# Four conditioning rows of the dense layer's scale summed by GpSimd, in a decoder trunk of two layers

## The reference, cut to what matters

```python
c_act = jax.nn.silu(c)
for l in range(DEPTH):
    mod = (c_act @ w_mod[l] + b_mod[l])[:, None, :]
    sh1, sc1, g1, sh2, sc2, g2 = jnp.split(mod, 6, axis=-1)
    h = x * (1.0 + sc1) + sh1
    y = hybrid_mixer(h, ...)
    x = layer_norm(DN_ALPHA * x + (1.0 + g1) * y, ln_g[l, 0], ln_b[l, 0])
    h = x * (1.0 + sc2) + sh2
    y = swiglu(h, ...) if l % 2 == 0 else moe_swiglu(h, ...)
    x = layer_norm(DN_ALPHA * x + (1.0 + g2) * y, ln_g[l, 1], ln_b[l, 1])
```

## Time and profile before

| what | value |
|---|---|
| median of 3 runs | 1275.26 us (1275.22 to 1275.42) |
| the profiled execution's own time | 1272.66 us |
| span of the profiled execution | 1270.9 us |
| granted TensorE clock, mean over the span | 0.983 |
| busy time of PE | 1183.0 us (93%) |
| busy time of DVE | 569.0 us (45%) |
| busy time of ACT | 302.1 us (24%) |
| busy time of POOL | 43.8 us (3%) |

### The profile page before, as it was taken

The page is one execution under the profiler, slowest core; times in us unless marked ns, Lnnn a source line. Parts: engine busy times, 40 slices in busy tenths (PEclk is TensorE's granted clock), DMA queues, the critical chain, the costliest instruction groups (busy, mean ns, idle before and its releaser), DMA issues.

```text
span 1270.9 us, 26228 instructions
## 1 busy us (share of the span) xinstructions
PE 1183.0 (93%) x11180; PEld 641.1 (50%) x11180; DVE 569.0 (45%) x913; ACT 302.1 (24%) x521; POOL 43.8 (3%) x84
## 2 busy tenths in 40 slices
PE   1889889999999898799999999999999999999996
PEld 1879867788878787523334323334233233333332
DVE  6799988677758999421021020111210210210224
ACT  0557243433336571310010010100100100100100
POOL 2101010000011010000000000000000000000001
PEclk9899989999999999799999999999999999999998
DMA  9973868899727648889999989999989999999950
GB/s 340 312 257 116 290 227 312 322 347 329 244 68 239 201 167 315 334 326 371 413 364 414 394 299 414 412 364 411 388 310 411 410 364 404 396 362 411 379 233 34
DMA packets 149083, 403.60 MB, mean 318 GB/s; under 512 B 19964, under 2 KB 71328, under 8 KB 137696
## 3 DMA queue, kind: packets, MB, share of 16 engines
q1 hardware_dynamic: 146720, 395.16, 82.5%
q0 software_dynamic: 2240, 6.68, 1.4%
HBM read 400.75 MB, written 1.05 MB: 316 GB/s over the span
## 4 chain that ended last, share of the span: by engine, by line
PE 75%; DVE 13%; DMA 6%; issue 3%; ACT 2%; SPq 1%; POOL 0%; DVEq 0%; ACTq 0%
PE bank L1349 36%; PE bank L1368 18%; PE bank L337 5%; PE bank L339 4%; PE bank L338 4%; DVE mod_acc L1541 3%; DMA raw_u<-in_ffn_w_up_dram 2%; DMA u_raw<-in_w_in_dram 2%; DVE u_low L1552 2%; PE bank L1331 1%; DMA mod_first<-in_w_mod_dram 1%; PE bank L1228 1%; DVE score L1596 1%; PE bank L1339 1%; PE bank L1022 1%
## 5 line engine op out<-in xcount | busy, mean ns | idle before, releaser
L1349 PE MATMUL bank<-raw_w,xg 128*32 128x512 f32 (+1 forms) x4608 | 462.9, 557 | 4.5 <-issue 2.5
L1349 PEld LDWEIGHTS bank<-raw_w,xg 128*32 128x32 f32 x4608 | 147.1, 110 | 304.7 <-issue 304.6
L1368 PE MATMUL bank<-raw_w,heT 128*32 128x512 f32 x2112 | 232.9, 593 | 0.0
L1915 DVE TENSOR_TENSOR he<-he,bank 128x256 f32<-128x256 f32 (+1 forms) x72 | 25.6, 384 | 369.4 <-ACT he L869 369.4
L869 ACT ACTIVATE he<-bank 128x256 f32<-128x256 f32 (+1 forms) x72 | 21.2, 367 | 542.8 <-PE bank L1349 542.8
L1368 PEld LDWEIGHTS bank<-raw_w,heT 128*32 128x32 f32 x2112 | 67.3, 110 | 150.5 <-issue 149.3
L1942 DVE SCALAR_TENSOR_TENSOR ycat<-bank,gate_tab,ycat 128x512 f32<-128x512 f32 x36 | 25.4, 747 | 173.0 <-PE bank L1340 171.1
L1541 DVE SCALAR_TENSOR_TENSOR mod_acc<-mod_row,c_act,mod_acc 128x1024 f32<-128x1024 f32 x70 | 89.8, 1283 | 6.8 <-DVE mod_acc L1541 0.9
L337 PE MATMUL bank<-u_high,hT_H 128*128 128x256 f32 x256 | 75.4, 294 | 4.9 <-DVE u_low L1552 3.5
L339 PE MATMUL bank<-u_high,hT_L 128*128 128x256 f32 x256 | 72.8, 284 | 0.0
L338 PE MATMUL bank<-u_low,hT_H 128*128 128x256 f32 x256 | 72.6, 284 | 0.0
(11 more groups left out here) (284 smaller groups left out, 1378.7 us busy)
## 6 DMA issues: line engine op xcount, KB each, us to landing
raw_w<-in_moe_w_down_dram SPq DMA_DIRECT2D x88, 1024.0 KB, 8.6
raw_w<-in_moe_w_gate_dram SPq DMA_DIRECT2D x128, 512.0 KB, 8.5
raw_w<-in_moe_w_up_dram SPq DMA_DIRECT2D x128, 512.0 KB, 9.8
mod_row<-in_w_mod_dram SPq DMA_DIRECT2D x80, 512.0 KB, 6.4
raw_w<-in_moe_w_gate_dram SPq DMA_DIRECT2D x64, 384.0 KB, 5.6
raw_w<-in_moe_w_up_dram SPq DMA_DIRECT2D x64, 384.0 KB, 6.8
u_raw<-in_w_in_dram SPq DMA_DIRECT2D x20, 1024.0 KB, 7.5
raw_d<-in_ffn_w_down_dram SPq DMA_DIRECT2D x11, 1024.0 KB, 10.1
```

What stands on the lines that cost most here:

```text
L1349: last = mm(bank[g][32 * q:32 * q + 32, 0:2 * HALF[c]].rearrange("s (m j r) -> s m j r", m=2, r=64), xg[:, i, k, 32 * g:32 * g + 32], cols ...
L1368: last = mm(bank[3 + g][32 * q:32 * q + 32, :], heT[(par + c) % 2][:, g, 2 * a + b, :], W[:, b, h * 512:(h + 1) * 512], start=(c == 0 and ...
L1915: V.tensor_tensor(h, h, bank[g][:, w:2 * w].rearrange("s (j c b) -> s j b c", b=2, c=32), ALU.mult).then_inc(s["m_hid"], 1)
```

## The change

GpSimd gets an accumulator of its own, `pool_acc`, of 128 x 1024, at a place where the first mixer keeps the attention probabilities and the dense layer its converted down weights. After the two RMS powers GpSimd waits until the second attention product has been made, and then takes rows 16 to 19: row 16 with one product by a scalar into `pool_acc`, rows 17 to 19 each with a product in place and a sum of two tiles. The product and the sum are separate instructions, with a semaphore between them.

VectorE leaves rows 16 to 19 out. Row 20 becomes the first of its accumulator (a product by a scalar) and counts for five rows in `row_rd`; rows 21 to 23 follow as before.

TensorE waits for the four rows of GpSimd before the scale's sum over partitions, and adds both accumulators there: 128 small products instead of 64, in pairs, the second of each pair added in PSUM.

SP waits, before it loads the weights of dense step 2 into `gu_in1`, also for the scale's sum over partitions (`mod_ps` at 4).

```diff
--- before.py
+++ after.py
@@ -84,6 +84,7 @@
 GATES = {2: 0, 9: 1, 10: 2, 11: 3}
 MOD_ROWS = [(m + FIRST_MOD, l, a, k) for m, (l, a) in enumerate(MODS) for k in range(KT)]
 ROWS_DENSE, ROWS_MIX1 = 24, 64
+POOL_ROWS = range(16, 20)
 ROWS_AT_STEP = (0, 5, 5, 5, 5, 4, 4, 4, 4, 4, 0)
 MOD_AT_STEP = {3: 5, 5: 6, 6: 7, 8: 8}
 
@@ -279,6 +280,8 @@
         last_S = place("last_S", [P, GROUPS, T], at=hTH_at)
         y_last = place("y_last", [P, GROUPS, 512], at=hfull_at)
 
+        pool_acc = place("pool_acc", [P, D], at=over + 40 * 1024)
+
         score, dsel, prob, relu = [score0, score1], [dsel0, dsel1], [prob0, prob1], [relu_a, relu_b]
 
         xH0 = place("xH0", [P, D], F32R, at=rows_at)
@@ -302,7 +305,7 @@
             yT_ps yT_H yT_L mv rstd x_n g3 stored
             f_guH f_guL f_gu f_silu f_hid f_t f_tH f_tL f_dH f_dL f_d
             rt_ps lg8 expd sel rank_ps npass lg_rd xb_ps xsplit xsplitL G xg_ps xg
-            m_used m_silu m_hid m_tH m_oS m_st m_S m_sc m_acc m_y0 m_y1 m_yH m_yL m_end""".split():
+            m_used m_silu m_hid m_tH m_oS m_st m_S m_sc m_acc m_y0 m_y1 m_yH m_yL m_end pool_rd""".split():
             s[name] = sem("s_" + name)
         row_ld = [sem(f"s_row_ld{i}") for i in range(NROWBUF)]
         mod_ld = row_ld + [sem(f"s_mod_ld{i}") for i in range(NROWBUF, len(FIRST_ROWS))]
@@ -442,6 +445,7 @@
                     sp.wait_ge(s["proj"], NU)
                 elif q == 2:
                     sp.wait_ge(s["row_rd"], 22)
+                    sp.wait_ge(s["mod_ps"], 4)
                 else:
                     sp.wait_ge(s["f_guL"], 2 * (q - 2))
                 b = (q + 1) % 2
@@ -604,6 +608,18 @@
             pool.wait_ge(s["mod_sum"], 2)
             gate_bias(0, 2, g_row)
             mixer(0)
+            pool.wait_ge(s["pv_ps"], 2)
+            for r in POOL_ROWS:
+                m, l, a, k = MOD_ROWS[r]
+                row = mod_row[0][ROW_BUF[r]]
+                pool.wait_ge(row_ld[ROW_BUF[r]], row_landed(r))
+                if k == 0:
+                    last = pool.tensor_scalar(pool_acc[:], row[:], c_act[:, 0:1], None, ALU.mult)
+                else:
+                    link(pool.tensor_scalar(row[:], row[:], c_act[:, k:k + 1], None, ALU.mult))
+                    pool.wait_ge(s["pool_rd"], k)
+                    last = pool.tensor_tensor(pool_acc[:], pool_acc[:], row[:], ALU.add)
+                last.then_inc(s["pool_rd"], 1)
             norm_power(0)
             gate_bias(0, 5, g_row)
             pool.wait_ge(s["x_ln"], 2)
@@ -980,10 +996,12 @@
             pe.wait_ge(s["stage_ld"], 32)
             nc.tensor.transpose(bank[7][:, 0:P], stage[:], ident[:]).then_inc(s["stageT"], 1)
 
-            def sum_chunk(acc, o):
+            def sum_chunk(acc, o, more=None):
 
                 for k in range(KT):
-                    last = mm4(o[:, k:k + 1], acc[:, k * P:(k + 1) * P], ones[:, 0:1], start=True, stop=True)
+                    last = mm4(o[:, k:k + 1], acc[:, k * P:(k + 1) * P], ones[:, 0:1], start=True, stop=more is None)
+                    if more is not None:
+                        last = mm4(o[:, k:k + 1], more[:, k * P:(k + 1) * P], ones[:, 0:1], start=False, stop=True)
                 return last
             pe.wait_ge(s["mod_sum"], 1)
             sum_chunk(ycat[:, 1, :], bank[6][:, KT:2 * KT])
@@ -1189,7 +1207,9 @@
                         if l == 0 and i == 2 + t:
                             m = i + 1
                             pe.wait_ge(s["row_rd"], (m - 1) * KT)
-                            sum_chunk(mod_acc[m % 2], bank[3 * t][:, 0:KT]).then_inc(s["mod_ps"], 1)
+                            if t:
+                                pe.wait_ge(s["pool_rd"], len(POOL_ROWS))
+                            sum_chunk(mod_acc[m % 2], bank[3 * t][:, 0:KT], pool_acc if t else None).then_inc(s["mod_ps"], 1)
                         elif l and t and i == 2:
                             pe.wait_ge(s["row_rd"], len(MOD_ROWS))
                             gate_sum(11, (0, 3))
@@ -1532,15 +1552,15 @@
                     row, acc = mod_row[int(n >= ROWS_MIX1)][ROW_BUF[n]], mod_acc[m % 2][:]
                     dve.wait_ge(row_ld[ROW_BUF[n]], row_landed(n))
                     if n:
-                        dve.wait_ge(s["row_rd"], n)
-                    if k == 0:
+                        dve.wait_ge(s["row_rd"], n if n - 1 not in POOL_ROWS else POOL_ROWS[0])
+                    if k == 0 or n - 1 in POOL_ROWS:
                         if m >= 4:
                             dve.wait_ge(s["mod_ps"], m - 2)
-                        last = V.tensor_scalar(acc, row[:], c_act[:, 0:1], None, ALU.mult)
+                        last = V.tensor_scalar(acc, row[:], c_act[:, k:k + 1], None, ALU.mult)
                     else:
                         last = V.scalar_tensor_tensor(out=acc, in0=row[:], scalar=c_act[:, k:k + 1], in1=acc,
                                                       op0=ALU.mult, op1=ALU.add)
-                    last.then_inc(s["row_rd"], 1)
+                    last.then_inc(s["row_rd"], 1 + len(POOL_ROWS) if n - 1 in POOL_ROWS else 1)
 
             def low_unit(l, u):
 
@@ -1750,7 +1770,7 @@
                 condition_rows(range(72, 76) if l else range(12, 16))
                 gate_apply(10 if l else 2, (1, 2), g_row)
                 low_unit(l, NIN + 3)
-                condition_rows(range(76, 80) if l else range(16, 24))
+                condition_rows(range(76, 80) if l else range(20, 24))
                 if l == 0:
                     dve.wait_ge(s["mod_ps"], 3)
                     conditioning(0, 3, bank[0][:, 0:KT]).then_inc(s["modT"], 1)
```

## The result

| | before | after |
|---|---|---|
| median of 5 runs | 1275.22 us | 1280.97 us |
| range of the runs | 1274.76 to 1275.42 | 1280.80 to 1284.34 |
| profiled execution, span | 1270.9 us | 1279.1 us |

The ratio is 1.0055, with a 95% interval of 1.0042 to 1.0068: slower by 5.4 to 8.7 us; 5.75 us between the medians, and 7.0 us by the ratio, which takes in that two of the five runs took 1284 us. I had forecast slower, by 3.4 us, and at most 5.2. The two spans lie 8.2 us apart, which is more than the medians do; single executions of the kernel before took from 1272 to 1279 us, so I read stages, and take off a shift of 0.39 us that the profile of after has before the stage begins.

What follows compares the result with a forecast made beforehand. VectorE's chain almost alone bounds the edited stage. Three products and three sums on its path, 3.2 + 6.3 - 0.5 - 5.56, give +3.4 us, small terms nothing: 1278.7 us on the median, range 1272.7 to 1280.4.

Steps and rivals of the forecast that it cites:

- VectorE's wait for the scale: Before tile 1: scale ready at 165.8, VectorE asks at 168.0, so hidden by 2.2 us and no wait.
- What is saved on VectorE: Scale's row steps on VectorE: four steps of 1.39 us go, 5.56 us saved.
- the rival without hindrance: GpSimd and VectorE don't hinder each other; TensorE's w_out end sets tile 1: -2.5 us, 1272.8; chance 0.22.
- the end of TensorE's products: Last w_out unit before the scale's sum: without hindrance TensorE's products are done at 160.4 and limit the gain.
- What its instructions cost: GpSimd's rows 16 to 19: four products of 1.06 us and three sums of 2.1 us, 10.5 us in all.
- Turns: VectorE and GpSimd alternate reading SBUF, whoever starts first holding the interface for its whole instruction: likeliest +3.4 us; chance 0.50.
- The small terms: Around the scale's sum: 64 more products (0.71 us) hidden; SP's wait, row 20's wait and GpSimd's queue cost nothing.
- SP's new wait: Before the load into gu_in1: scale's sum at 165.8 precedes SP's arrival at 167.2, so it costs nothing.
- The rest of the program: Behind the edited stage, from TensorE's last dense product on: nothing found that would absorb a few microseconds.
- VectorE always wins: Rival: VectorE isn't delayed, GpSimd's last sum ends near 166, tile 1 starts at 168.1: +3.0 us, 1278.3; chance 0.08.
- a quick sum: Rival: GpSimd's sum of two tiles takes 1.06 us like its product: +0.3 us, 1275.6; chance 0.18, shared with partial hindrance.

Runs made afterwards that it cites:

- run 5: The change without GpSimd's part and the sum's second half, rows 16 to 19 left out of the scale; against the kernel before, ratio 0.9974, -3.3 us.
- run 1: The kernel before once more, no edit, with a second profile; its span was 1273.4 us, 2.5 us over the first.
- run 2: Kernel before with VectorE and TensorE unchanged, GpSimd making the four products and three sums for nobody; ratio 1.0063, +8.0 us.
- run 3: Kernel before with GpSimd making seven fills of 128 x 1024 beside VectorE instead of products and sums; ratio 1.0000.
- run 9: The change with both accumulators summed by halves, so TensorE has as many products as the kernel before; against that kernel, ratio 1.0026, +3.3 us.
- run 6: The change with two rows (16 and 17) on GpSimd instead of four; against the kernel before, ratio 1.0031, +4.0 us.
- run 8: The kernel before with TensorE adding `mod_acc` twice in the scale's sum; ratio 1.0017, +2.2 us.
- run 4: The kernel before with two products by a scalar and two sums of two tiles at GpSimd's start, on own tiles; one execution took 1276.36 us.
- run 12: Against the kernel before: rows 16 and 17 on TensorE by halves, shift and scale summed by halves, scale's sum between tile 1's w_out units; ratio 0.9970, -3.8 us.

## Why the prediction was wrong

The direction was right, the size not: +5.75 us between the medians (7.0 by the ratio, interval 5.4 to 8.7) against +3.4, and above my range by 0.6. Two terms that I had put at nothing make up the difference: VectorE's wait for the scale, and the experts' loop.

*What is saved on VectorE:* right. In run 5 row 12 to the end of row 23 took 13.81 us instead of 19.25, 5.44 less, with 0.22 us of waiting for row 23 instead of a step's 0.1. Its -3.3 us meets the -2.5 of the rival without hindrance with 0.7 us of the sum off, but partly by luck: the end of TensorE's products, which I had fixed at 160.4, moved by 1 us there, and it moves by as much between two traces of the kernel before (run 1).

*What its instructions cost:* both mis-sized. The sum is 2.34 us for my 2.1. The product is 2.87 us for my 1.06, which I took from the rate of the affine select; 18.5 us of work instead of 10.5, so GpSimd ended at 165.1.

*Turns:* right in kind (runs 2 and 3), and nearly in size: VectorE lost 8.3 us for my 9.0. The product's length and hold are different things: it holds VectorE for 0.7 us only, where I charged nearly all of its 1.06 (and the fourth, beside row 20, for 0.85). Two errors met, and that the total came out near is luck: an instruction nearly three times as long, and a hold of two thirds of what I charged. The last sum then ran beside tile 0's residual instead of a row. The net +3.4 of this term stands against +2.8 in the trace up to tile 0's statistics and +3.3 (1.9 to 4.6) in run 9.

*The small terms:* here it failed. I had the scale's sum "ready at 165.8", hidden by 2.2 us, since 64 products more take 0.71 us. They took about that (127 of the 128 in 1.2 us), and then TensorE stood still for 2.39 us. With the products' later end (165.1 for 164.3; the 72 took 11.4 us at a granted clock of 0.74, where my sum had 10.3) the scale came at 169.0 and VectorE waited 1.33 us. SP's new wait did bind, but by little: the load into gu_in1 was issued at 169.10, 4.0 us behind the w_out products, where run 9, with its sum long over, issued it 3.6 us behind them. What these 0.4 us cost is open.

*The rest of the program:* not in my sum at all. "I find nothing behind it that would absorb a few microseconds" asked what would take the loss away, not what would add to it. The 64 counted products more, ahead of the experts' loop, cost 2.3 us inside it. Three kernels with 11244 counted products (the change, runs 6 and 8) have the step, 2.3 to 2.7 us over the two passes; those with 11180 (the kernel before and runs 1, 2, 3, 4, 5, 9 and 12) stay within -0.3 and +0.6 us of the kernel before. Kernels with 11436 have none either, and the one with 11148 gains 1.5 us a pass and loses 2.4 later. So more products don't simply cost more; that it is the place of the loop in TensorE's program is argued, not shown. That the loss comes from how instructions are fetched is a likely reading of "issue"; no trace here shows it, so it stays open.

*The rivals:* that VectorE always wins is out (it lost 8.3 us), no hindrance is out, and a quick sum is out (2.34 us).

## What to carry to other kernels

Work given to GpSimd isn't free time: if it reads SBUF while VectorE adds SBUF tiles, a sum of two tiles takes its length from VectorE, and the sum over partitions that joins the halves is new work too; count how many microseconds VectorE gets back for each that it loses (here 5.56 for 8.3). If rows are to leave VectorE, the engine that waits at that moment is the one to take them, in products of a size that ran without a stall (here by halves). And a change of a few dozen instructions ahead of a loop should be timed against a version with the same count, or whatever the shift does to the loop is timed with it.

## What the runs showed that I had not expected

- GpSimd's product by a scalar from SBUF, 128 x 1024 in float32, takes 2.87 us alone, longer than its sum of two tiles (2.34), and holds a two-input VectorE instruction back by 0.67 to 0.68 us only.
- TensorE's products with one column start 11 ns apart by quarters (64 in 0.71 us), 29 ns by halves, 110 ns whole; by quarters the engine stood still for 2.3 to 5.2 us after 127 to 134 on end in three kernels, and not at all after 128 in two others (runs 6 and 8).
- A fill by GpSimd under a VectorE product by a scalar took 1.49 us instead of 0.95, with no effect on VectorE.
- 64 counted products more in TensorE's program cost 2.2 us (0.6 to 3.6) in run 8 with their own time hidden.
- The same 72 w_out products ran at a granted clock of 0.84 in one trace of the kernel before (10.3 us) and of 1.00 in the other (run 1, 8.9 us), so a term taken from them in one trace is uncertain by 1.5 us.
